# Six input tiles in three passes, an earlier softplus and norm rows in partition halves, in a two-block transformer kernel

## The chip, the cores and the metric

One core of one Trainium2 chip runs the whole program. The metric is the device time in microseconds (us) of one launch, as the median of several runs; lower is better. Engines are called by their short names: PE is TensorE (PEld its weight loads), DVE is VectorE, ACT is ScalarE, POOL is GpSimd, and SP issues the DMAs of the weights. Every engine works through its own list of instructions in program order; a semaphore holds one back until another engine is done.

## What is computed

Two transformer blocks on 256 tokens of width 1024, all in float32. The change touches only the mixer of the second block. Cut to what matters:

```python
u = _rms(h, ln_mix_g)
p = u @ w_in                                   # 1024 x 3384
p_rwkv, p_mla, p_gdn = _split(p, (RWKV_IN, MLA_IN, GDN_IN))
y = concat([rwkv7_time_mix(p_rwkv, ...),       # 6 heads of 64
            mla_attention(p_mla, ...),         # 4 "latent" heads, 96 wide, softmax
            gated_deltanet(p_gdn, ...)])       # 6 heads of 64
h = h + y @ w_out

# in gated_deltanet
q, k, v = split(silu(causal_conv4(qkv)))       # q, k, v from nine input tiles of 128 columns
q, k = l2norm(q) * HEAD_DIM ** -0.5, l2norm(k) # per head and token
g = -exp(a_log) * softplus(a + dt_bias)        # the step sizes, 6 heads x 256 tokens
o = chunked_delta_rule(q, k, v, beta, g)
o = _rms(o, o_norm_g) * silu(gate)             # per head and token
```

The rwkv part has two more such norms per head and token: of its keys (`kk`) and of its output (a group norm).

## The kernel before, in words

**Products.** A product of float32 operands is made in one of two ways. `product_f` (its matmuls are line 626) multiplies the float32 weights with the float32 operand directly, eight matmuls per tile of 128 columns; the profile shows two records for each. `product3` (line 669) works on operands that were split before into a high and a low part of type fp32r: high by high, high by low, low by high, 24 matmuls per tile. The high part is made by an ACT copy, the low part by a DVE subtraction. Most weights are split in pieces (`split_high`, line 1645, and `split_low`, line 2217). The operand of the second block's input product is split too (`stream2`, IN_HIGH and IN_LOW), but its last chunks, in2 3 to 6, are used unsplit.

**The latent heads.** The four softmax heads (units NU to NU+3) run in a loop over u with the names below. What each engine does for step u, in its order:
- PE: `scores` of head u (L798), `probs_T` of head u-1 (three transposes, L839), `filler`, one input tile of chunks in2 4 and 5 (`product_f`, 128 columns, eight matmuls), and `values` of head u-1 (L845 to L847). Fillers 0 to 5 stand in front of and in this loop; tiles 6 and on follow behind it.
- ACT: the conv's first tap of a finished tile (L1695, with a copy of the tile, L1666), `take_probs_T` (L1794), `exps` (L1784, two Exp with sums), `conv_tanh` (L1703); at u = NU, NU+1, NU+2 a step of the softplus on 6x256 or 6x128 numbers: Exp (L2008), Ln (L2011), two Exp (L2014).
- DVE: `bias_scores` (L2379, L2381), `conv_taps` (three, L2261), `conv_out` (L2270), `finish_head` (L2420), and `delta_rule_rows`, which is the DVE's side of the softplus (L2721, L2722, L2726, then L2729 to L2733 with two scans); at u = NU also `key_factors` (L2746 to L2753).

Each engine's list is written out by hand; buffers are double (`u % 2`), so DVE waits for ACT's tap and tanh and ACT for DVE's mask within a step.

**Behind the loop.** `kk_r` are the norm factors of the keys, spread over the heads' rows by PE (`spread_rows`, L1146) and multiplied in by DVE (L2772). DVE then goes through decay factors, conv tiles and the first matrices of the triangular inverse without a break up to the masks of `by_k` (L2981); PE's `removed_values` (L1227) waits for these. From there the inverse runs level by level: PE makes products "p" (L1384), ACT copies them (L1718), PE makes "t", DVE adds (L2825) and transposes (L2832). Between p and t of a level stands `part(lv)`: for the rwkv inverse `spread_rows` of the norms of q and k (levels 2 and 3, DVE L2870 and L2876); after level 4 of the second inverse, `gn_r`.

**Norm rows.** A norm is: squares; `row_sums` (L1095), which sums each head's 64 rows with six matmuls of 32 output rows, three for tokens 0 to 127 into rows 0 to 31 and then three for tokens 128 to 255 into rows 32 to 63; a Sqrt on ACT (L1973) and a reciprocal on DVE; `spread_rows`, six matmuls from 64 rows, which place the factors on 128 rows again, tile by tile.

**The output product.** Fills and jobs are PSUM banks with a fixed order. `out2(dc, tt, ks)` adds the products of the mixer's eight tiles k (0 to 2 rwkv, 3 and 4 latent, 5 to 7 delta rule) for token half tt and column half dc. Tiles 5 to 7 exist last: DVE multiplies by `o_r` (L3013), ACT makes the high parts (L2134), DVE the low parts (L3007), tile by tile; out2(0, ...) takes k = 4 to 7 with both token halves under each k.

## Time and profile before

| | us |
|---|---|
| runs, median of 3 (lowest, highest) | 958.39 (958.37, 959.28) |
| profiled execution, its own time | 958.64 |
| its span from the first to the last instruction | 956.8 |
| PE busy, matmuls (PEld, weight loads) | 935.7 (829.5) |
| DVE busy | 589.0 |
| ACT busy | 471.9 |
| POOL busy | 61.9 |
| mean granted TensorE clock, share of full | 0.998 |
| the latent heads' loop and what follows up to L1227 | about 610 to 669 |
| the levels of the two inverses | about 666 to 741 |
| output product of the mixer | about 741 to 774 |

Busy is the time in which the engine works on an instruction; the times of the span count from its start. A line of the timeline gives the start, the duration (of a whole run of like instructions, where it ends in a count), and in brackets how long the engine had stood idle before, with what released it.

### The profile page before, as it was taken

The page shows a single profiled execution, that of the slowest core. Times are in us where ns is not written, and L with a number is a line of the kernel's source. Part 1 is how long each engine was busy: PE and PEld are TensorE (multiplying, and loading weights), DVE is VectorE, ACT ScalarE, POOL GpSimd, SP SyncE. Part 2 cuts the span into 40 slices and gives each one's busy share as a digit, 9 for nine tenths or more (in the row PEclk, how much of TensorE's full clock was granted, in tenths as well). Part 3 has the DMA queues.
Part 4 walks back from the last instruction along what each step waited for, and adds up shares of the span by engine and source line. Part 5 has one row for each costly group of instructions (what it writes and reads, how often), then busy time and mean ns, then how long its engine had stood idle before and what let it go on. Part 6 is the DMA issues. An engine that isn't in the chain of part 4 may idle for free.

```text
span 956.8 us, 16842 instructions
## 1 busy us (share of the span) xinstructions
PE 935.7 (98%) x7117; PEld 829.5 (87%) x7117; DVE 589.0 (62%) x933; ACT 471.9 (49%) x709; POOL 61.9 (6%) x78
## 2 busy tenths in 40 slices
PE   6999999999999999999999999999999999999998
PEld 5999987787778789999988889887988789998886
DVE  4775445557678755555544669578767466665434
ACT  5644335546774445444453584556336455454331
POOL 1000000020002300000000000002350000000000
PEclk9999999999999999999999999999999999999999
DMA  9985552234346534444554432222000444455521
GB/s 354 202 323 186 192 197 103 107 123 163 131 174 257 189 149 177 177 176 177 185 193 172 182 132 113 89 89 89 3 2 12 167 177 176 177 186 199 215 104 45
DMA packets 14778, 149.86 MB, mean 157 GB/s; under 512 B 1696, under 2 KB 3872, under 8 KB 6128
## 3 DMA queue, kind: packets, MB, share of 16 engines
q1 hardware_dynamic: 12448, 139.65, 39.3%
q0 software_dynamic: 1296, 5.24, 2.9%
q10 hardware_dynamic: 960, 3.90, 1.1%
q8 instruction: 57, 0.93, 0.4%
q14 instruction: 17, 0.14, 0.0%
HBM read 144.59 MB, written 4.19 MB: 155 GB/s over the span
## 4 chain that ended last, share of the span: by engine, by line
PE 83%; DVE 7%; ACT 4%; issue 2%; POOL 1%; ACTq 0%; DVEq 0%; POOLq 0%
PE bank L669 63%; PE bank L626 5%; PE bank L1384 3%; DVE W_LOW L2217 3%; ACT W_HIGH L1645 2%; PE bank L798 1%; POOL HN L3102 1%; PE bank L839 1%; PE bank L876 1%; PE bank L1146 1%; DVE ARENA L2261 1%; DVE X L2523 1%; PE bank L1251 1%; DVE OUT_LOW L2217 0%; PE bank L635 0%
## 5 line engine op out<-in xcount | busy, mean ns | idle before, releaser
L2217 DVE TENSOR_TENSOR W_LOW<-weights,W_HIGH 128x2048 fp32r<-128x2048 f32 (+1 forms) x98 | 224.4, 2292 | 212.2 <-ACT W_HIGH L1645 212.2
L1645 ACT ACTIVATE W_HIGH<-weights 128x2048 fp32r<-128x2048 f32 (+1 forms) x98 | 186.7, 1907 | 262.9 <-PE bank L669 262.9
L669 PE MATMUL bank<-OVER_HT,W_HIGH 128*128 128x256 f32 x608 | 171.0, 281 | 0.3 <-DVE OVER_HN L2229 0.3
L669 PE MATMUL bank<-OVER_HN,W_HIGH 128*128 128x256 f32 x608 | 170.5, 280 | 0.0
L669 PE MATMUL bank<-OVER_HT,W_LOW 128*128 128x256 f32 x608 | 170.5, 280 | 0.0
L669 PEld LDWEIGHTS bank<-OVER_HT,W_HIGH 128*128 128x128 f32 x608 | 114.5, 188 | 1.0 <-issue 0.7
L669 PEld LDWEIGHTS bank<-OVER_HN,W_HIGH 128*128 128x128 f32 x608 | 114.5, 188 | 0.0
L669 PEld LDWEIGHTS bank<-OVER_HT,W_LOW 128*128 128x128 f32 x608 | 114.5, 188 | 0.0
L669 PE MATMUL bank<-W_LOW,HID_HIGH 128*128 128x512 f32 x200 | 77.9, 389 | 0.0
L669 PE MATMUL bank<-W_HIGH,HID_LOW 128*128 128x512 f32 x200 | 77.8, 389 | 0.0
L669 PE MATMUL bank<-W_HIGH,HID_HIGH 128*128 128x512 f32 x200 | 77.8, 389 | 0.0
L669 PE MATMUL bank<-FIRST_HIGH,W_HIGH 128*128 128x256 f32 x224 | 63.6, 284 | 2.0 <-DVE W_LOW L2217 1.4
L669 PE MATMUL bank<-FIRST_HIGH,W_LOW 128*128 128x256 f32 x224 | 63.4, 283 | 0.0
L669 PE MATMUL bank<-FIRST_LOW,W_HIGH 128*128 128x256 f32 x224 | 63.3, 283 | 0.0
L626 PE MATMUL bank<-HT,weights 128*128 128x256 f32 x240 | 55.4, 383 | 0.0
L669 PE MATMUL bank<-GATE_HIGH,FIRST_HIGH 128*128 128x512 f32 x128 | 52.5, 410 | 0.5 <-DVE RING_LOW L2357 0.5
L669 PE MATMUL bank<-RING_LOW,FIRST_HIGH 128*128 128x512 f32 x128 | 50.3, 393 | 0.0
L626 PEld LDWEIGHTS bank<-HT,weights 128*128 128x128 f32 x240 | 44.5, 190 | 6.7 <-issue 0.7
L669 PE MATMUL bank<-GATE_HIGH,FIRST_LOW 128*128 128x512 f32 x128 | 50.2, 392 | 0.0
L2357 DVE TENSOR_TENSOR RING_LOW<-weights,GATE_HIGH 128x1024 fp32r<-128x1024 f32 x32 | 40.7, 1271 | 11.9 <-ACT GATE_HIGH L1680 11.9
L669 PEld LDWEIGHTS bank<-FIRST_HIGH,W_HIGH 128*128 128x128 f32 x224 | 42.3, 189 | 3.4 <-DVE W_LOW L2217 1.8
L669 PEld LDWEIGHTS bank<-W_HIGH,HID_HIGH 128*128 128x128 f32 x200 | 37.5, 188 | 7.8
(513 smaller groups left out, 1873.7 us busy)
## 6 DMA issues: line engine op xcount, KB each, us to landing
weights<-weights_dram SPq DMA_DIRECT2D x63, 2048.0 KB, 8.0
bias_rows_dram<-ARENA POOLq DMA_DIRECT2D x1, 3072.0 KB, 40.5
weights<-weights_dram SPq DMA_DIRECT2D x2, 1024.0 KB, 5.8
BIAS<-params_dram ACTq DMA_DIRECT2D x1, 1997.0 KB, 14.3
weights<-weights_dram SPq DMA_DIRECT2D x1, 1664.0 KB, 6.6
weights<-weights_dram SPq DMA_DIRECT2D x1, 1584.0 KB, 6.8
X<-x_dram ACTq DMA_DIRECT2D x2, 512.0 KB, 4.4
HT<-bias_rows_dram POOLq DMA_DIRECT2D x1, 1024.0 KB, 9.9
```

Of the source, the lines that this page charges most:

```text
L626: ins = pe.matmul(o, w[:, k, a:a + n], HT[:, k, :], start=(k == 0), stop=(k == KD - 1))
L669: ins = pe.matmul(o, left[a][k], right[b][k], start=(first and k == 0 and a + b == 0), stop=(last and k == n - 1 and a == 1))
L798: ins = pe.matmul(BK[4 + u % 2][:, c0:c1], q[:, q0:q0 + P], k[:, 0:n], start=True, stop=(br != 2))
L839: ins = pe.transpose(probsT_bank(u)[:, j * P:(j + 1) * P], PB_[:, u % 2, j * P:(j + 1) * P], ident)
L876: ins = pe.matmul(o[pb:pb + HD, c0:S], V[:, n, a:a + HD], PT_[:, u % 2, k0:k1], start=(n == 0), stop=(n == 1))
L1146: ins = pe.matmul(o[:, c * P:(c + 1) * P], at[0:HD, :], rows, start=True, stop=True)
L1251: ins = pe.matmul(o[pb:pb + HD, c * P:(c + 1) * P], a[:, c, h * HD:(h + 1) * HD], b[:, matrix(c, h), :], start=(n == 0), stop=(c == 0 and ...
L1384: ins = pe.matmul(o[b:b + HD, n * HD:(n + 1) * HD], left[b:b + HD, 4 * g + n, :], right[b:b + HD, 4 * g + n, :], start=True, stop=True)
L1645: act.activation(like_source(piece_parts(k)[0], k), piece_source(k), ACT.Copy).then_inc(sem("pieces_high"), 1)
L2217: dve.tensor_tensor(low, piece_source(k), high.bitcast(F32), ALU.subtract)\
L2261: ins = dve.scalar_tensor_tensor(out=a, in0=o[:, 0:S - d], scalar=w[tap], in1=a, op0=ALU.mult, op1=ALU.add)
L2357: dve.tensor_tensor(low, src, high.bitcast(F32), ALU.subtract).then_inc(sem("gate_split"), 1)
```

## The change

**Tiles.** Input tiles 0 to 5 of chunks in2 4 and 5 (fillers 0 to 5) are made by `product3`. For tile n ACT copies the high part into one of two buffers TILE_HIGH0 and TILE_HIGH1 (`tile_high`, 128x1024), DVE writes the low part over the weights themselves (`tile_low`, 128x1024, into RING_LOW). Tiles 0 and 1 are split in front of the loop, tiles 2 to 5 at the head of steps 0 to 3: tile n + 2 waits until PE has read tile n.

**Softplus.** Both first steps of the softplus (DVE rows and Exp, Ln) move in front of the loop, followed by an Exp on one number.

**Norm rows.** Sums take 64 output rows per token half, in turns between the halves; the root and the reciprocal work on 128 rows; `spread_rows` reads token half c from rows 64c to 64c+63 and writes it to a bank of its own, in turns between the two. The DVE instructions that use the factors go by token halves (128x3x128) and not by tiles. One ACT copy that made a second set of selectors goes away; one of 32x384 remains.

**Output product.** `o_r` is used by token halves: two multiplications, two high parts, two low parts. out2(0, ...) takes k = 4 for both token halves, then k = 5 to 7 for the first and then for the second.

```diff
+        IN_TILES = 6
+        TILE_HIGH = [over("TILE_HIGH0", "HN", 0, [KD, P]), over("TILE_HIGH1", "BIAS", Y_RW_AT, [KD, P])]
...
             def row_sums(o, src):
-                for c in range(2):
-                    for t in range(3):
-                        ins = pe.matmul(o[32 * c:32 * c + 32, :], HEADS[:, 32 * t:32 * t + 32], src[:, t, c * P:(c + 1) * P],
+                for t in range(3):
+                    for c in range(2):
+                        ins = pe.matmul(o[HD * c:HD * (c + 1), :], HEADS[:, HD * t:HD * (t + 1)], src[:, t, c * P:(c + 1) * P],
                                         start=(t == 0), stop=(t == 2))
...
-                ins = product_f(o[:, t * S:(t + 1) * S], w, (n % 4) * P)
+                if n < IN_TILES:
+                    pe.wait_ge(sem("tiles_split"), n + 1)
+                    ins = product3(o[:, t * S:(t + 1) * S], [[part[:, k, :] for k in range(KD)] for part in in_tile(n)[0:2]],
+                                   [[part[:, k, :] for k in range(KD)] for part in stream2])
...
             def spread_rows(names, rows):
-                for o, t, last in tile_slots(names):
-                    for c, at in enumerate((prm2("pair_rows", t * P, P), LATE_ROWS[:, t * P:(t + 1) * P])):
-                        ins = pe.matmul(o[:, c * P:(c + 1) * P], at[0:HD, :], rows, start=True, stop=True)
+                banks = open_halves(*names)
+                for t in range(3):
+                    for c, o in enumerate(banks):
+                        half = slice(c * HD, (c + 1) * HD)
+                        ins = pe.matmul(o[:, t * P:(t + 1) * P], prm2("pair_rows", t * P, P)[half], rows[half],
+                                        start=True, stop=True)
...
-            for k in range(4, KD):
-                for tt in range(TT):
-                    out2(0, tt, (k,))
+            for tt in range(TT):
+                out2(0, tt, (4,))
+            for tt in range(TT):
+                out2(0, tt, range(5, KD))
...
             def tile_high(n):
+                slot, turn = weight_slots("in2", 4 + n // 4)
+                act.wait_ge(sem(f"weights_in{slot}"), 16 * turn)
+                if n >= 2:
+                    wait_tile_read(act, n - 2)
+                high, _, src = in_tile(n)
+                act.activation(high[:, :, :], src, ACT.Copy).then_inc(sem("tiles_high"), 1)
...
             act.activation(BETA, BETA, ACT.Tanh, scale=0.5).then_inc(sem("beta_tanh"), 1)
+            act.wait_ge(sem("sp_minus_abs"), 2)
+            act.activation(GSPT, GSPT, ACT.Exp).then_inc(sem("sp_exp"), 1)
             for n, dst in enumerate((QTm, KTm)):
                 for b in range(2):
                     take_fill(("mla_T", 2 * n + b), flat(dst[0:QK, 2 * b:2 * b + 2, :]), 512, rows=QK)
+            act.wait_ge(sem("sp_exp1"), 2)
+            act.activation(GSPT, GSPT, ACT.Ln).then_inc(sem("sp_ln"), 1)
+            act.activation(SPARE, SMALL[0], ACT.Exp)
             for u in range(NU, NU + MH + 1):
+                if u < NU + IN_TILES - 2:
+                    tile_high(u - NU + 2)
...
+            delta_rule_rows(NU)
+            delta_rule_rows(NU + 1)
             for u in range(NU, NU + MH + 1):
                 if u < NU + MH:
                     bias_scores(u)
+                if u < NU + IN_TILES - 2:
+                    tile_low(u - NU + 2)
...
+            for c in range(2):
+                o = fill_arrived(dve, ("o_r", c))
+                fill_out(dve.tensor_tensor(token_half(Y_GD, c), token_half(GKB, c), three_tiles(o), ALU.mult), ("o_r", c))
+            for c in range(2):
+                dve.wait_ge(sem("y2_high"), 3 + c)
+                dve.tensor_tensor(token_half(OVER_HT[:, 5:8, :], c), token_half(Y_GD, c),
+                                  token_half(OVER_HN[:, 5:8, :], c).bitcast(F32), ALU.subtract).then_inc(sem("y2_split"), 1)
```

The order of instructions on ACT between the tanh of beta (L1991 before, L2035 in the change) and the first two Exp with sums of the loop (L1784 before, L1818 in the change), first before, then in the change. L1718 and L1752 are the copies of the transposed queries and keys:

```order
L1991 ACTIVATE SM<-SM 6x256 [waits beta_in]
L1718 ACTIVATE ARENA<-bank 96x512 [waits fills_written] x4
L1784 ACTIVATE ARENA,STAT<-ARENA,STAT 128x128 [waits probsT_written,scores_read]
L1784 ACTIVATE ARENA,STAT<-ARENA,STAT 128x256
L2008 ACTIVATE SM<-SM 6x256 [waits sp_minus_abs]
```

```order
L2035 ACTIVATE SM<-SM 6x256 [waits beta_in]
L2037 ACTIVATE SM<-SM 6x256 [waits sp_minus_abs]
L1752 ACTIVATE ARENA<-bank 96x512 [waits fills_written] x4
L2042 ACT_TABLE_LOAD
L2042 ACTIVATE SM<-SM 6x256 [waits sp_exp1]
L2043 ACT_TABLE_LOAD
L2043 ACTIVATE STAT<-STAT 128x1
L2021 ACTIVATE TILE_HIGH_57<-weights 128x1024 [waits tiles_read,weights_in1]
L1818 ACTIVATE ARENA,STAT<-ARENA,STAT 128x128 [waits probsT_written,scores_read]
L1818 ACTIVATE ARENA,STAT<-ARENA,STAT 128x256
```

Two table loads, the Ln, the one-number Exp and the high part of tile 2 now stand ahead of the first head's exponentials; before, both loads came in the loop's steps 1 and 2.

DVE at the start of the loop, before and in the change. The two ISA rows that name a bank are the masks of a head's scores (L2379 and L2381 before, L2425 and L2427 in the change), RECIPROCAL is the first instruction of `key_factors`:

```order
L2379 ISA ARENA,STAT<-bank,CST 128x128 [waits job_out0,probs_ready,scores_written,residual_scaled]
L2379 ISA STAT 128x1
L2381 ISA ARENA,STAT<-bank,CST 128x256
L2381 ISA STAT 128x1
L2721 TENSOR_SCALAR SM<-SM 6x256 [waits beta_tanh]
L2722 SCALAR_TENSOR_TENSOR SM<-SM 6x256
L2746 RECIPROCAL HN<-HN 64x128 [waits fill_out4]
```

```order
L2775 TENSOR_SCALAR SM<-SM 6x256 [waits job_out0,beta_tanh,residual_scaled]
L2776 SCALAR_TENSOR_TENSOR SM<-SM 6x256
L2780 TENSOR_SCALAR SM<-SM 6x256 [waits sp_exp]
L2425 ISA ARENA,STAT<-bank,CST 128x128 [waits probs_ready,scores_written]
L2425 ISA STAT 128x1
L2427 ISA ARENA,STAT<-bank,CST 128x256
L2427 ISA STAT 128x1
L2759 TENSOR_TENSOR RING_LOW_50<-weights,TILE_HIGH_57 128x8x128 [waits tiles_high]
L2800 RECIPROCAL HN<-HN 128x128 [waits fill_out4]
```

The low part of tile 2 stands between the first head's masks and `key_factors`, and waits for ACT's high part; the same instruction, for tiles 3 to 5, stands behind the masks of heads 1 to 3.

## Rows read from the trace of the kernel before

**Rows 1.** The page: busy time of each engine, and the chain that ended last, by engine.

```profile
PE 935.7 (98%) x7117; PEld 829.5 (87%) x7117; DVE 589.0 (62%) x933; ACT 471.9 (49%) x709; POOL 61.9 (6%) x78
PE 83%; DVE 7%; ACT 4%; issue 2%; POOL 1%; ACTq 0%; DVEq 0%; POOLq 0%
```

**Rows 2.** Stretches: length, busy us (xcount) of PE, PEld, DVE, ACT, POOL; clock, DMA, GB/s.

```profile
615.00:641.00 26.00, 26.00 (x147) 23.31 (x146) 19.46 (x60) 14.86 (x39) 0.00 (x0) 1.00 0.25 95
641.00:668.00 27.00, 26.05 (x250) 21.94 (x248) 24.07 (x52) 17.18 (x39) 5.59 (x8) 1.00 0.22 79
684.00:700.00 16.00, 16.00 (x275) 14.70 (x275) 12.50 (x31) 9.18 (x21) 5.93 (x6) 0.89 0.01 2
```

**Rows 3.** Timeline of PE: start us, us, engine line op out<-in xcount [idle before <-releaser].

```profile
668.96 1.62 PE L1227 MATMUL bank<-HN,ARENA 128*64 128x64 f32 x48 [1.29 <-DVE ARENA L2981]
```

**Rows 4.** Timeline of PE: a product_f tile (16 records), and product3 matmuls 24 apart.

```profile
614.98 3.62 PE L626 MATMUL bank<-HT,weights 128*128 128x256 f32 x16
...
583.25 0.28 PE L669 MATMUL bank<-IN_LOW,W_HIGH 128*128 128x256 f32 x1
...
586.13 0.28 PE L669 MATMUL bank<-IN_LOW,W_HIGH 128*128 128x256 f32 x1
```

**Rows 5.** One line each: 128x1024 high and low parts elsewhere; then two low parts on end.

```profile
L1680 ACT ACTIVATE GATE_HIGH<-weights x32: 1040/1057/1063, 136.2 to 270.5; 128x1024 fp32r<-128x1024 f32 x32
L2357 DVE TENSOR_TENSOR RING_LOW<-weights,GATE_HIGH x32: 1214/1224/1776, 139.2 to 274.4; 128x1024 fp32r<-128x1024 f32 x32
...
768.68 4.48 DVE L2217 TENSOR_TENSOR W_LOW<-weights,W_HIGH 128x2048 fp32r<-128x2048 f32 x2
```

**Rows 6.** Timeline of ACT: copies before the loop, and the softplus's Ln between two table loads.

```profile
610.96 2.00 ACT L1718 ACTIVATE ARENA<-bank 96x512 f32<-96x512 f32 x4
...
622.77 1.28 ACT L2011 ACT_TABLE_LOAD   x1
624.40 0.42 ACT L2011 ACTIVATE SM<-SM 6x256 f32<-6x256 f32 x1 [0.35 <-DVE SM L2726]
...
625.86 1.28 ACT L1784 ACT_TABLE_LOAD   x1
```

**Rows 7.** Timeline of DVE in the loop of the latent heads and just behind it.

```profile
615.28 0.29 DVE L2379 CUSTOM_DVE_ANT_0 ARENA<-bank,CST 128x128 f32<-128x128 f32 x1 [4.74 <-PE bank L798]
...
616.04 0.40 DVE L2722 SCALAR_TENSOR_TENSOR SM<-SM 6x256 f32<-6x256 f32 x1
...
628.48 0.42 DVE L2270 SCALAR_TENSOR_TENSOR ARENA<-ARENA 128x256 f32<-128x256 f32 x1 [1.74 <-ACT ARENA L1703]
...
632.36 1.52 DVE L2261 SCALAR_TENSOR_TENSOR ARENA<-ARENA,BIAS 128x255 f32<-128x255 f32 x3 [1.07 <-ACT ARENA L1695]
...
639.40 1.14 DVE L2772 TENSOR_TENSOR ARENA<-ARENA,bank 128x512 f32<-128x512 f32 x2 [0.59 <-PE bank L1146]
```

**Rows 8.** Timeline of PE and DVE around spread_rows of the norms of q.

```profile
673.45 0.49 PE L1146 MATMUL bank<-HN,BIAS 64*128 64x128 f32 x2
...
674.98 3.02 PE L1384 MATMUL bank<-ARENA 64*64 64x64 f32 x96
...
674.64 1.02 DVE L2870 SCALAR_TENSOR_TENSOR ARENA<-ARENA,bank 128x512 f32<-128x512 f32 x2 [1.05 <-PE bank L1146]
```

**Rows 9.** Timeline of PE: other matmuls from 64-row halves, four of 128 and twelve of 256.

```profile
653.73 0.71 PE L1183 MATMUL bank<-ARENA 64*128 64x128 f32 x8 [0.61 <-ACT HN L1718]
...
663.26 2.86 PE L1211 MATMUL bank<-ARENA 64*128 64x256 f32 x24
```

**Rows 10.** Timeline: row_sums of the delta rule's output; the reciprocal of gn_r on DVE.

```profile
756.05 1.09 PE L1095 MATMUL bank<-ARENA,NF 128*32 128x128 f32 x12
...
726.75 0.94 DVE L2945 RECIPROCAL HN<-HN 64x128 f32<-64x128 f32 x1 [1.32 <-ACT HN L1973]
```

**Rows 11.** Timeline of DVE and PE in the output product.

```profile
761.24 0.75 DVE L3013 TENSOR_TENSOR HT<-ARENA,bank 128x256 f32<-128x256 f32 x2 [2.72 <-PE bank L1146]
...
767.62 0.50 PE L669 MATMUL bank<-OUT_HIGH,OVER_HN 128*128 128x512 f32 x1 [0.18 <-DVE OUT_LOW L2217]
```

More of the change, by code:

```diff
@@ L430, in wait_job_out, with in_tile, wait_tile_read @@
             eng.wait_ge(sem(f"job_out{j % 4}"), j // 4 + 1)
+        def in_tile(n):
+            slot = weight_slots("in2", 4 + n // 4)[0]
+            cols = slice(n % 4 * P, (n % 4 + 1) * P)
+            src, low = [t[:, :].rearrange("p (k n) -> p k n", k=KD)[:, :, cols] for t in (rings[slot], RING_LOW[slot])]
+            return TILE_HIGH[n % 2], low, src
+        def wait_tile_read(eng, n):
+            if n % 2:
+                eng.wait_ge(sem("jobs_written"), JOB_AT["in2", 4 + n // 4, n // 2 % 2] + 1)
+            else:
+                eng.wait_ge(sem("tiles_read"), n // 2 + 1)
         def piece_parts(k):
@@ L2708, in _, with tile_low @@
             ins.then_inc(sem("rates_low"), 1)
+            def tile_low(n):
+                dve.wait_ge(sem("tiles_high"), n + 1)
+                high, low, src = in_tile(n)
+                dve.tensor_tensor(low, src, high[:, :, :].bitcast(F32), ALU.subtract).then_inc(sem("tiles_split"), 1)
             shift_tiles(3, 0, (8, 9))
+            for n in range(2):
+                tile_low(n)
             shift_tiles(3, 1, (10,))
```

95 lines of the change are left out of this document (42 added, 53 removed).

## The prediction, made before the kernel was run

> **What bounds the kernel now.** I read the page first. PE is busy for 98% of the span and holds 83% of the chain that ended last [rows 1], so a microsecond taken off PE should count, unless another engine is as full in that place. So I read each stretch by itself. In the latent heads' loop (615 to 641) PE is never idle and DVE is busy 19.46 of 26 us, with 6.5 us idle in small waits. Behind it (641 to 668) DVE is busy 24.07 of 27 [rows 2], and at its end PE stands still for 1.29 us until DVE has masked the `by_k` matrices [rows 3]. So from the loop to L1227 both engines are nearly full, and the last wait ends on DVE: PE time saved there is worth only what DVE can follow. The change takes work off PE and puts new work on DVE and ACT in just this place. From L1227 on PE leads again: DVE waits 1.05 us for `spread_rows` [rows 8].
>
> **Tiles, the PE side.** A `product_f` tile takes 3.62 us [rows 4]. In `product3` 24 matmuls start within 2.88 us (583.25 to 586.13), the last ending 0.16 later than the step: 3.04 us. Saved: 0.58 a tile, 3.5 for six.
>
> **Tiles, the DVE and ACT side.** A high part of 128x1024 takes ACT 1.06 us, a low part DVE 1.22 [rows 5]; two low parts on end take 4.48 where one of 2.28 is listed, so the next starts 0.1 before the end, and I take 1.13 a low part. Tiles 0 and 1 fall into idle time in front of the loop (DVE then waits 4.74 us for the first scores [rows 7]) and cost nothing; if they did delay anything it would be by their 2.3 us, but 4.74 covers them. Tiles 2 to 5 add 4 x 1.13 = 4.5 us to DVE within the loop.
>
> **Softplus.** Three DVE rows leave the loop, the longest 0.40 us [rows 7]; I take 0.85 for all (0.2 to 1.2). On ACT the Exp now comes before the four copies and waits for the tanh and two DVE rows: copies that began at 610.96 [rows 6] begin about 0.9 later and end at 613.9. Then come a table load (1.28), Ln (0.35), a table load (1.28) and the small Exp (0.1): 616.9, and with tile 2's high part (1.06) 617.95. In front of the loop the shorter `row_sums` gives 0.2 and tile 0 0.6, but PE's first scores need the copies, so DVE's loop starts only 0.2 us earlier than at 615.28. Its masks are done at 615.6, and it waits until 617.95 for the high part: a **new wait of 2.35 us**, with `key_factors` and the next head's masks queued behind it, for which ACT's second exponentials and then PE's `probs_T` wait.
>
> **The loop, as DVE's account.** From the first masks to the keys' norms are 24.1 us (615.28 to 639.40 [rows 7]). Out: rows -0.85; the wait of 1.74, which is the table loads of Ln in steps 1 and 2, back to the usual 0.5 for a tanh, -1.2; the 1.07 for a tap, -1.05; the 0.59 for `spread_rows`, -0.6, since PE is ahead of DVE there; two small waits for PE and ACT, -0.65. In: low parts +4.5; the wait at tile 2 +2.35; at tile 5 about +1.35, because its high part stands on ACT behind two Exp (size of the Ln's 0.42 [rows 6]) that wait for DVE's scans, so 0.8 + 1.06 less the 0.55 us of masks. Sum +3.85, less the 0.2 at the start: +3.65. From there to L1227 DVE has no slack, except that the product of `by_k` is waited for less, as PE gains on DVE: -0.45. **To L1227: +3.2 us.** PE's 3.5 saved become idle time, mostly in front of `probs_T` and `values`. Bounds: 2.3, if each signal costs 0.04 less than I count; 4.3 with the full 1.22 and 1.06.
>
> **Norm rows.** No row shows six 128-column matmuls in turns between row halves. Four (L1183) take 0.71 us, 0.35 a pair. Twelve of 256 columns (L1211), six pairs, take 2.86, 0.48 a pair, so a pair of 128 columns would take 0.24 [rows 9]. Three pairs: 0.7 to 1.05; I take 0.88, nearer to the value of L1183, as three short pairs are more like two than like six of double length. Now it takes 1.53 (673.45 to 674.98 [rows 8]), so 0.65 less each (0.45 to 0.8; zero if the halves do not run side by side). `gq_r` and `gk_r`: 1.3, less 0.2 as DVE's share of a level (its 1.02 for the factors and two groups of three) becomes the longer at the second: -1.1. `gn_r`: DVE arrives through ACT's table load and root (its wait of 1.32 is on ACT [rows 10]) and has no idle time behind it, so half counts: -0.3. `kk_r` is in the account above. TensorE: Matmul & The Clock Gate of the Trainium skill (section on array packing by 32x32 tiles) has small-K matmuls in distinct row groups run fully side by side; three pairs would then take about 0.65 (its rule with the 0.2 that a matmul of 128 columns takes alone, an estimate), and the sum would be 0.7 us lower than mine; the trace agrees only in part, with 0.35 and 0.24 a pair.
>
> `row_sums`: 1.09 us now [rows 10] in 32-row outputs; I take 0.2 less for the turns (0 to 0.45), which counts at the last one only; the others are covered by DVE, or by ACT's root. Root, reciprocal and the halved DVE instructions have as many elements per row and cost what they did. One ACT copy of 32x384 and a larger memset on POOL lie before the loop, where POOL has nothing else and ACT waits; I count nothing for them, and 0.4 at most if ACT were full there. SP's next loads wait for the same jobs as before and are for the output product, some 100 us later: nothing.
>
> **Output product.** PE reaches it 0.85 us earlier (0.2 + 0.65). It now needs tile k = 5 of the first token half 1.5 us after `spread_rows`; the chain DVE 0.47, ACT 0.42, DVE 0.5 and three signals is 1.75, so PE waits some 0.2. The 0.18 for the last low part [rows 11] goes, because ACT has two high copies rather than three in front of it. Sum -0.9 (-0.3 to -1.2). If the chain is longer, the work hidden now behind four matmul groups shows.
>
> **The sum.** +3.2 - 1.1 - 0.3 - 0.9 = **+0.9 us**. The profiled execution took 958.64, 0.25 above the median of 958.39; from the median: **959.3 us**. About 0.2% (1.9 us) is what a measurement of this kernel can tell from no change, so this reads as none.
>
> **Rivals.**
> *PE leads in the loop after all* (chance 0.2). If DVE's low parts fit into its 6.5 idle us [rows 2] and the wait at tile 2 does not come, each of steps 0 to 4 is shorter by PE's 0.58, and L1227 comes 3.1 earlier: 959.3 - 3.2 - 3.1 = 953.0. For it: PE's share of the page, and enough idle time by number. Against: the idle pieces are round trips with ACT that stay, and the loads stand in front of tile 2.
> *Slower: the halves do not run side by side* (0.13). If three pairs take as long as six matmuls (1.53), or DVE proves the longer in the levels too, the 1.1, 0.3 and 0.65 of 0.9 are lost, 2.05 in all, and the 3.2 stand: 961.4. It decides from about 1.4 us for three pairs. For it: two pairs of L1183 are 40% dearer than long ones. Against: L1211.
> *The clock falls* (0.12). In 684 to 700 the granted clock is 0.89 of 2.4 GHz on average [rows 2], that is 3.5 us at the 1.2 GHz level, 1.75 us of work, with PE busy throughout. PE will now stand still for over 3 us in step 3. One such stretch more in a place where PE leads costs 1.75: 961.05; inside the loop, DVE covers it. If the stretch at 694 goes instead, the same amount is gained (957.5, which reads as no change; I give it a third of this chance).
> *Dearer table loads* (0.05). In the trace Ln follows 1.63 us after the start of its load, 0.35 of it a wait for DVE, so a switch costs 1.28 [rows 6]; the loads of the first step then cost 2.56 and the wait 2.35. If a switch took twice that, the new wait would be 4.9 and the time 961.9. ScalarE: Activation LUTs of the Trainium skill (What ACT_TABLE_LOAD costs) gives 1.38 us of draining beside 1.28 of loading per switch, 2.66 together; that would be 962.1, and the trace disagrees.
> *The rest*, 0.5, is my forecast, with its own range 957.6 to 961.2 from the bounds above.
>
> **Chances.** Faster by over 0.2% (below 956.5): the first rival and the edge of mine, 0.22. Slower (above 960.3): the halves 0.13, the clock 0.08, the table loads 0.05 and 0.1 of mine, 0.36, put at 0.35. Same: the rest, 0.43. The range has to leave out 0.2: that is the first rival in full. Its low end, 955.6, lies a little under the middle between 959.3 and 953.0, for a loop in which PE leads in some steps only; its high end is the dearest of the others, 961.9.
>
> **What would show it.** Right: a DVE wait of 2 to 3 us for TILE_HIGH before the first `key_factors`, one of about 1.3 before the last; the keys' norms (L2772's place) 3 to 4 us later than 639.40; L1227 about 3.2 us later, still released by DVE; PE idle several us in the loop; `spread_rows` 0.8 to 1.0 us long; the output product starting about 1.8 later than before and its end 0.9. Wrong: L1227 earlier than 668.96; a DVE wait under 1 us at tile 2; PE without idle time in the loop; or `spread_rows` at 1.5.

## The result, and the profile after

| | before | after |
|---|---|---|
| runs, median (lowest, highest), 18 each | 958.52 us (956.93, 960.95) | 960.69 us (959.01, 962.94) |
| ratio, 95% interval | | 1.0021 (1.0013 to 1.0029) |
| profiled execution (span) | 958.64 us (956.8) | 960.36 us (958.5) |

The change makes the kernel slower by 0.21%, 2.0 us by the ratio (2.2 between the medians); the interval, 0.13 to 0.29%, lies about the bound of 0.2% for "no change". The forecast was 959.3, +0.9 us.

The page of the changed kernel, busy time and chain, against [rows 1]:

```profile
PE 930.4 (97%) x7165; PEld 825.1 (86%) x7165; DVE 595.9 (62%) x937; ACT 476.7 (50%) x714; POOL 62.1 (6%) x78
PE 79%; DVE 10%; ACT 6%; issue 3%; POOL 1%; ACTq 0%; DVEq 0%; POOLq 0%
```

PE lost 5.3 us of work and 4 points of the chain; DVE and ACT, which gained 6.9 and 4.8 us, took them over. The stretches, with the columns of [rows 2]:

```profile
615.00:641.00 26.00, 21.13 (x146) 19.68 (x145) 20.48 (x52) 14.67 (x38) 0.00 (x0) 0.88 0.22 82
641.00:668.00 27.00, 26.02 (x215) 22.18 (x216) 22.35 (x45) 17.48 (x39) 4.41 (x6) 0.99 0.21 79
684.00:700.00 16.00, 16.00 (x317) 14.70 (x314) 12.29 (x31) 8.51 (x19) 4.50 (x4) 1.00 0.01 3
```

In the loop PE is idle for 4.9 of 26 us, where it was never idle, and its clock is 0.88: a part of the loop runs at the 1.2 GHz level. The low stretch that the kernel before had behind 694 us is gone here.

**A common zero first.** The two profiles part before the first changed instruction. A table load of ACT behind a long run of `product3` matmuls, and a read of DVE at the head of the part that this case is about, first before, then after:

```profile
486.46 1.28 ACT L1584 ACT_TABLE_LOAD   x1
570.30 0.16 DVE L2628 TENSOR_SCALAR STAT<-bank 128x2 f32<-128x2 f32 x1 [1.36 <-PE bank L1040]
```

```profile
485.04 1.28 ACT L1618 ACT_TABLE_LOAD   x1
568.90 0.16 DVE L2674 TENSOR_SCALAR STAT<-bank 128x2 f32<-128x2 f32 x1 [1.89 <-PE bank L1063]
```

The profiled execution after is 1.40 us ahead at 570, by work that is the same in both. A second step of this kind lies behind 780 us (last section), so the ends of two spans can't be compared either. Therefore, below, "against before" means the difference of the times of one and the same instruction, plus 1.40; for other kernels, plus what they were ahead at this read.

Timeline of DVE after, through the loop, against [rows 7]:

```profile
613.71 0.29 DVE L2425 CUSTOM_DVE_ANT_0 ARENA<-bank,CST 128x128 f32<-128x128 f32 x1 [2.78 <-PE bank L821]
...
616.75 1.23 DVE L2759 TENSOR_TENSOR RING_LOW<-weights,TILE_HIGH 128x1024 fp32r<-128x1024 f32 x1 [2.40 <-ACT TILE_HIGH L2021]
...
633.88 1.23 DVE L2759 TENSOR_TENSOR RING_LOW<-weights,TILE_HIGH 128x1024 fp32r<-128x1024 f32 x1 [1.18 <-ACT TILE_HIGH L2021]
...
642.70 0.17 DVE L2466 RECIPROCAL STAT<-STAT 128x2 f32<-128x2 f32 x1 [1.75 <-PE bank L870]
...
643.56 1.14 DVE L2831 TENSOR_TENSOR ARENA<-ARENA,bank 128x384 f32<-128x384 f32 x2 [0.37 <-PE bank L1178]
```

The first masks come 0.17 earlier against before (613.71 - 615.28 + 1.40 = -0.17; forecast 0.2). The waits at tiles 2 and 5 are 2.40 and 1.18 (forecast 2.35 and 1.35). The third wait, 1.75 for L870, the values of head 3, is not in the forecast, and the keys' norms are 5.56 late (643.56 - 639.40 + 1.40) where 3.65 were forecast. Timeline of PE around that wait, and the same time in stretches of 2 us (columns of [rows 2]):

```profile
635.10 0.69 PE L868 MATMUL bank<-ARENA 128*128 128x64 f32 x2 [2.87 <-ACT ARENA L1828]
635.59 0.63 PE L869 MATMUL bank<-ARENA 128*128 128x64 f32 x2
...
637.94 0.41 PE L692 MATMUL bank<-IN_LOW,TILE_HIGH 128*128 128x256 f32 x1
...
641.88 0.33 PE L868 MATMUL bank<-ARENA 128*128 128x64 f32 x2
```

```profile
632.00:634.00 2.00, 0.23 (x2) 0.02 (x1) 0.82 (x6) 1.81 (x4) 0.00 (x0) 1.00 0.71 303
634.00:636.00 2.00, 0.90 (x4) 0.90 (x5) 1.97 (x3) 1.93 (x7) 0.00 (x0) 0.66 0.00 0
636.00:638.00 2.00, 2.00 (x12) 2.00 (x12) 1.45 (x6) 1.09 (x3) 0.00 (x0) 0.50 0.00 0
638.00:640.00 2.00, 2.00 (x11) 2.00 (x11) 1.86 (x5) 0.18 (x1) 0.00 (x0) 0.50 0.00 0
640.00:642.00 2.00, 2.00 (x14) 2.00 (x13) 0.46 (x2) 0.42 (x1) 0.00 (x0) 0.63 0.04 8
```

PE stood still for 2.87 us in front of the values of head 2. While it did, the clock fell to 1.2 GHz and stayed there until about 641.4. Tile 5 then took 4.94 us (636.94 to 641.88) instead of some 3.0, a matmul of 128x256 0.41 instead of 0.28, and the values of head 3 behind it came when DVE had long been ready. What PE had waited for is in ACT's list:

```profile
632.19 0.41 ACT L2059 ACTIVATE SM<-SM 6x256 f32<-6x256 f32 x1 [2.35 <-DVE SM L2787]
632.51 0.39 ACT L2060 ACTIVATE SM<-SM 6x128 f32<-6x128 f32 x1
632.81 1.04 ACT L2021 ACTIVATE TILE_HIGH<-weights 128x1024 fp32r<-128x1024 f32 x1
...
634.59 0.46 ACT L1828 ACTIVATE ARENA<-bank 128x384 f32<-128x384 f32 x1
```

L1828 copies the transposed probabilities of head 2. In front of it stand two Exp that wait for DVE's scans and the high part of tile 5.

Behind the loop: PE at L1260 (L1227 before, [rows 3]), and at the norms of q (L1178, [rows 8]); DVE's factors for q; the output product [rows 11].

```profile
672.91 1.62 PE L1260 MATMUL bank<-HN,ARENA 128*64 128x64 f32 x48 [1.29 <-DVE ARENA L3037]
...
677.40 0.94 PE L1178 MATMUL bank<-HN,BIAS 64*128 64x128 f32 x12
678.27 3.17 PE L1417 MATMUL bank<-ARENA 64*64 64x64 f32 x96
...
765.25 0.47 PE L692 MATMUL bank<-OUT_HIGH,OVER_HN 128*128 128x512 f32 x1 [0.35 <-DVE OVER_HT L3066]
```

```profile
678.37 1.02 DVE L2928 SCALAR_TENSOR_TENSOR ARENA<-ARENA,bank 128x384 f32<-128x384 f32 x2 [0.82 <-PE bank L1178]
...
741.70 2.29 DVE L2263 TENSOR_TENSOR OUT_LOW<-weights,OUT_HIGH 128x2048 fp32r<-128x2048 f32 x1
...
766.83 2.29 DVE L2263 TENSOR_TENSOR OUT_LOW<-weights,OUT_HIGH 128x2048 fp32r<-128x2048 f32 x1 [1.26 <-ACT OUT_HIGH L1679]
```

L1260 is still released by DVE, with the same wait of 1.29. `spread_rows` takes 0.87 us for 1.53. From the keys' norms on, the lead of the kernel before shrinks: 5.56 at the norms, 5.35 at L1260, 3.92 at the split at 741.70 (739.18 before) and 2.96 at that of 766.83 (765.27 before).

### The profile page after: what moved, and what is told of

Its sections match the earlier page's. It is cut to its first block, busy times and chain, and to the rows that moved or that the text cites. A ratio compares the mean times of both kernels' runs of the same rounds, so it can differ in the third digit from the quotient of the medians.

```text
span 958.5 us, 16955 instructions
## 1 busy us (share of the span) xinstructions
PE 930.4 (97%) x7165; PEld 825.1 (86%) x7165; DVE 595.9 (62%) x937; ACT 476.7 (50%) x714; POOL 62.1 (6%) x78
## 4 chain that ended last, share of the span: by engine, by line
PE 79%; DVE 10%; ACT 6%; issue 3%; POOL 1%; ACTq 0%; DVEq 0%; POOLq 0%
PE bank L692 63%; PE bank L1417 3%; DVE W_LOW L2263 3%; PE bank L649 2%; ACT W_HIGH L1679 2%; DVE ARENA L2307 1%; POOL HN L3150 1%; PE bank L821 1%; PE bank L862 1%; PE bank L899 1%; DVE X L2569 1%; PE bank L1284 1%; DVE OUT_LOW L2263 0%; PE bank L1178 0%; PE bank L658 0%
## 5 line engine op out<-in xcount | busy, mean ns | idle before, releaser
L692 PEld LDWEIGHTS bank<-W_HIGH,HID_LOW 128*128 128x128 f32 x200 | 37.5, 188 | 7.9
L692 PEld LDWEIGHTS bank<-W_LOW,HID_HIGH 128*128 128x128 f32 x200 | 37.5, 188 | 7.9
```

Source lines behind the costliest of these rows:

```text
L692: ins = pe.matmul(o, left[a][k], right[b][k], start=(first and k == 0 and a + b == 0), stop=(last and k == n - 1 and a == 1))
```

## The experiments

Twelve kernels were run, each timed in five rounds beside the kernel before, four at a time on one chip. Each is the changed kernel with an edit. Two times of each profile are in this table, both "against before" as above: DVE's product just behind the keys' norms (640.58 before), and its split of an output piece (739.18 before). The last columns say where a profile shows the clock below 0.9, and the ratio of the times.

```
kernel                    640.58   739.18   clock low at     ratio (95%)
norm_rows_only            -0.44    -2.07    -                0.9975 (0.9965 to 0.9986)
norm_rows_softplus        -0.31    -0.63    694-702          0.9972 (0.9962 to 0.9982)
two_tiles                 -0.93    -2.55    694-698          0.9976 (0.9966 to 0.9986)
two_tiles_softplus_back   -1.39    -1.58    702-706          0.9962 (0.9949 to 0.9975)
reordered4                -0.62    -2.25    -                0.9977 (0.9968 to 0.9987)
reordered                 +1.90    +0.27    636-640          0.9990 (0.9982 to 0.9999)
high2_early               +1.96    +0.53    634-638, 696-700 0.9999 (0.9990 to 1.0007)
softplus_back             +2.53    +2.33    628-636, 706-710 1.0011 (1.0002 to 1.0019)
five_tiles                +4.00    +2.38    634-638          1.0011 (1.0001 to 1.0021)
pe_kept_busy              +3.27    +3.13    706-710          1.0011 (1.0003 to 1.0020)
tiles_parts_unused        +3.49    +1.86    -                1.0022 (1.0012 to 1.0032)
the change                +5.56    +3.92    634-642          1.0021 (1.0013 to 1.0029)
norm_rows_undone          +5.96    +7.44    634-642, 710-714 1.0050 (1.0032 to 1.0067)
```

### Which part costs: norm rows alone, with the softplus, with six tiles

```diff
-        IN_TILES = 6
+        IN_TILES = 0
...
-            act.wait_ge(sem("sp_minus_abs"), 2)
-            act.activation(GSPT, GSPT, ACT.Exp).then_inc(sem("sp_exp"), 1)
...
-            act.wait_ge(sem("sp_exp1"), 2)
-            act.activation(GSPT, GSPT, ACT.Ln).then_inc(sem("sp_ln"), 1)
-            act.activation(SPARE, SMALL[0], ACT.Exp)
...
-                if u == NU + 2:
+                if u == NU:
+                    act.wait_ge(sem("sp_minus_abs"), 2)
+                    act.activation(GSPT, GSPT, ACT.Exp).then_inc(sem("sp_exp"), 1)
+                elif u == NU + 1:
+                    act.wait_ge(sem("sp_exp1"), 2)
+                    act.activation(GSPT, GSPT, ACT.Ln).then_inc(sem("sp_ln"), 1)
+                elif u == NU + 2:
...
-            delta_rule_rows(NU)
-            delta_rule_rows(NU + 1)
...
-                if u > NU + 1:
-                    delta_rule_rows(u)
+                delta_rule_rows(u)
```

> The changed kernel with no split tile (all input tiles by product_f) and the softplus back in the loop: what is left is the norm rows and the output product. By my account these are worth 0.5 us at the keys' norms (the 0.59 that DVE waited for spread_rows), 1.1 at the norms of q and k, 0.3 at gn and 0.65 in the output product: 2.5 us below the kernel before, about 956.0, with no clock below 2.4 GHz in the loop. If the row halves do not gain (the rival), it is within 0.5 us of before. If the step of 1.4 us between 355 and 486 us, in code that the change does not touch, belongs to the changed program and not to the execution, this profile shows it too; if it belongs to the execution, it is there or not by chance.

Measured: 956.54 us, ratio 0.9975, 2.4 us faster. The norm rows and the output product are worth what the account gave them. The zero of this profile is 0.15, so the 1.40 of the change's profile does not come with the norm rows.

`norm_rows_softplus` has `IN_TILES = 0` alone and keeps the softplus in front.

> As the run before, but with the softplus in front of the loop. By my account DVE loses 0.85 us of rows and 1.2 us of a wait for the Ln's table loads in the loop, and the two loads stand in front of the first exponentials, which come about 0.9 us later: 0.5 to 1.5 us faster than the run with the norm rows alone, about 955.0. If the loads in front cost as much as those in the loop, no difference.

Measured: 956.04 us, ratio 0.9972, no measurable difference to the run before; at the keys' norms it is 0.13 later. The expected gain did not come: DVE's waits for the Ln are gone, but it then waits 1.11 and 1.41 us for values of PE. The rival held.

`softplus_back` has the other hunks and keeps six tiles.

> The changed kernel with the softplus back in the loop, six tiles split. Account: the wait of 2.35 us at tile 2 goes, the rows (0.85) and the wait for the Ln (1.2) come back: within 0.5 us of the changed kernel (960.2 to 961.2) if the clock falls as before, and about 958.5 if ACT's other order keeps PE from standing still for 2.9 us in front of the values of head 2, so that the clock does not fall. The rival that the table loads are what makes the change slow expects 958 as well, but with an idle PE and a low clock still there.

Measured: 959.69 us, ratio 1.0011, about 1 us below the change, between the cases. PE still stood idle, 2.31 us, one step earlier, and the clock fell there. In this place DVE did cover the fall: none of its waits up to the keys' norms is for PE. What it waits for is ACT, whose Ln and its table load now hold up the high part of tile 4 (1.11 us), and tile 5 (1.18).

```profile
628.06 0.69 PE L868 MATMUL bank<-ARENA 128*128 128x64 f32 x2 [2.31 <-ACT ARENA L1828]
```

The last of the parts, all but the norm rows and the output product:

```diff
             def spread_rows(names, rows):
-                banks = open_halves(*names)
-                for t in range(3):
-                    for c, o in enumerate(banks):
+                for o, t, last in tile_slots(names):
+                    for c, at in enumerate((prm2("pair_rows", t * P, P), LATE_ROWS[:, t * P:(t + 1) * P])):
...
```

> The changed kernel with the norm rows and the output product as they were: six split tiles and the softplus in front remain. Theory (the parts add up: norm rows and output product are worth 2.4 us, tiles with softplus cost the rest): 2.0 to 2.5 us above the changed kernel, about 0.45% above before (962.5 to 963.2). The profile should show the same DVE waits at tiles 2 and 5, PE idle for about 2.9 us and the low clock behind it. Rival (the change's parts interact, and the norm rows' gain came from what the loop left open): within 1 us of the changed kernel.

Measured: 963.23 us, ratio 1.0050, 2.8 us above the change. `spread_rows` of q takes its old 1.53 us. The parts add up: norm rows and output product bring 0.25% alone and 0.29% here (1.0050 to 1.0021); six tiles with the softplus cost 0.46% on top of them (0.9975 to 1.0021) and 0.50% by themselves. The profile has DVE's waits at tiles 2 and 5 (2.39 and 1.18), PE's idle time (2.87) and the low clock behind it, as expected.

### Is it PE's idle time and the clock

In `pe_kept_busy` PE repeats tile 4's product behind tile 4:

```diff
                 filler(u - NU + 1)
+                if u == NU + 3:
+                    product3(job_bank(("in2", 5, 0))[:, S:2 * S], [[part[:, k, :] for k in range(KD)] for part in in_tile(4)[0:2]],
+                             [[part[:, k, :] for k in range(KD)] for part in stream2])
```

> The changed kernel, with 24 more matmuls behind tile 4, which fill the 2.87 us in which PE waited for ACT's copy in front of the values of head 2; they repeat tile 4's product into the half of the bank that tile 5 then writes over, so the result is unchanged. Theory (the clock fell after this idle time, tile 5 then took 4.9 us instead of 3.0 and DVE waited 1.75 us for the values of head 3): granted clock 1.0 throughout the loop, the wait of 1.75 below 0.3, time 1.5 to 2.0 us below the changed kernel (958.7 to 959.2). Rival (DVE's own work sets the end of the loop and the wait is only taken over by the next one): clock 1.0 but a time within 0.5 us of the changed kernel.

Measured: 959.93 us, ratio 1.0011, about 1.0 us below the change, less than expected. In the loop the theory held. The clock is 1.0, DVE does not wait for the values of head 3, and the keys' norms come 2.3 us earlier than in the change; timelines of DVE and PE:

```profile
640.56 0.33 PE L868 MATMUL bank<-ARENA 128*128 128x64 f32 x2
...
642.22 0.16 DVE L2469 RECIPROCAL STAT<-STAT 128x2 f32<-128x2 f32 x1
```

In this profile the rest went behind 706 us, where it has a low stretch that the change's has not. The first table prices it: from 640.58 to 739.18 every profile without a low stretch in between gains 1.62 to 1.64 us (norm_rows_only, reordered4, reordered, five_tiles, tiles_parts_unused, the change), and the four with one beyond 700 only 0.14 to 0.32. So a stretch there costs 1.3 to 1.5 us. One that is over by 700 costs 0.2 (`high2_early`) or nothing (`two_tiles`; the kernel before has its own in the same place), as DVE leads there. But the stretch at 706 is not why the kernel gained only 1.0 us: its five executions at a mean clock of 1.000 have a median of 960.47, its six at 0.998 one of 959.52. Executions at full clock lie 2.8 us apart here (957.93 to 960.74), which is more than a fall costs. The two speeds of the last section can make up to 2.4 us of that; which execution had which, only a trace would tell. So the gain in time that the theory forecast, 1.5 to 2.0 us, is not shown, though its mechanism in the loop is.

Second, in `tiles_parts_unused` ACT and DVE do all of their splitting, but tiles 2 to 5 are `product_f` again, over the low parts (so this part of the output is not the reference's):

```diff
-                    ins = product3(o[:, t * S:(t + 1) * S], [[part[:, k, :] for k in range(KD)] for part in in_tile(n)[0:2]],
-                                   [[part[:, k, :] for k in range(KD)] for part in stream2])
+                    if n < 2:
+                        ins = product3(o[:, t * S:(t + 1) * S], [[part[:, k, :] for k in range(KD)] for part in in_tile(n)[0:2]],
+                                       [[part[:, k, :] for k in range(KD)] for part in stream2])
+                    else:
+                        low = in_tile(n)[1].bitcast(F32)
+                        ins = product_f(o[:, t * S:(t + 1) * S], low, 0)
```

> The changed kernel, where tiles 2 to 5 are multiplied by product_f again, as before, while ACT and DVE make their high and low parts all the same (the product is taken with the low parts, so this part of the output is not the reference's). PE has 4 x 0.58 = 2.3 us more work in the loop, ACT's and DVE's lists are unchanged. Theory (PE's saving within the loop buys nothing, since DVE sets the time there and the saved time is idle time that also lets the clock fall): no slower than the changed kernel, and 0.5 to 1.5 us faster if the idle time of 2.87 us shrinks so far that the clock stays at 2.4 GHz. Rival (PE's work counts in the loop): 1 to 2.3 us slower than the changed kernel, 961.5 to 963.

Measured: 960.19 us, ratio 1.0022, the change's within the noise. PE does 2.3 us more in the loop, and it costs nothing that the times show. Its profile is the change without a low clock:

```profile
635.09 0.43 PE L868 MATMUL bank<-ARENA 128*128 128x64 f32 x2 [2.29 <-ACT ARENA L1832]
```

```profile
641.04 0.29 DVE L2471 TENSOR_TENSOR NF<-bank,STAT 128x128 f32<-128x128 f32 x1
...
641.48 1.14 DVE L2835 TENSOR_TENSOR ARENA<-ARENA,bank 128x384 f32<-128x384 f32 x2
```

DVE's list up to the masks of head 3 is that of the change (its waits at tiles 2 and 5 are 2.40 and 1.19), and the keys' norms are 3.49 late instead of 5.56: the clock's share of the change's loop is 2.07 us by this pair of profiles, 2.29 by that of `pe_kept_busy`. The theory also expected a faster kernel, and it is not: its other executions fell about as often as the change's. This table has the mean granted clock of every timed execution (0.999 counted with 1.000; before, in the three sets that ran beside the experiments); 0.998 is about one stretch of some 3.5 us at half speed in 957, 0.996 two or a longer one:

```
                        executions   1.000   0.998   under 0.998
before (three sets)             83      49      24            10
the change                      18       0       4            14
tiles_parts_unused              12       2       3             7
high2_early                     11       1       2             8
softplus_back                   11       0       4             7
norm_rows_undone                 6       1       2             3
reordered                       11       1       8             2
five_tiles                      12       1       8             3
pe_kept_busy                    12       5       6             1
norm_rows_only                   7       5       2             0
norm_rows_softplus               7       3       3             1
two_tiles                        9       4       4             1
reordered4                      12       6       3             3
two_tiles_softplus_back          6       3       3             0
```

No execution of the change kept its clock, and 14 of 18 lost the longer time; before, 10 of 83, of which 8 in the set of 23 that ran beside `tiles_parts_unused`. In the change the executions under 0.998 have a median of 961.3, the four at 0.998 one of 959.4; in `tiles_parts_unused` those under 0.998 have 961.3, the others 959.6. So sorted by clock the two kernels take the same time, and the clock is worth some 1.7 to 2.0 us in both. The profiled execution of `tiles_parts_unused` (959.23, its fastest) is one of its two clean ones. Where in the span the others fell, no trace shows. A profile of one execution shows where a fall may be and what it costs, not how often it comes.

### Places against amount

> The changed kernel with IN_TILES = 2: only tiles 0 and 1, whose parts are made in front of the loop; norm rows and softplus as in the change. Theory (the tiles split within the loop are what costs: their low parts and the two waits for high parts, and the clock after PE's idle time; tiles 0 and 1 are free): the time of the run with norm rows and softplus alone (956.0) less 0.6 for tile 1, since tile 0 only makes PE wait for ACT's copies: about 955.5. Rival (splitting as such is dear, by ACT and DVE time in front of the loop too): 956.5 or more.

The edit of `two_tiles` is `IN_TILES = 2`. Measured: 956.21 us, ratio 0.9976: 4.3 us below the change, so what costs is in tiles 2 to 5; the other two are not dear, but the 0.6 that the profile shows at the keys' norms did not come through in the times.

```diff
+            tile_high(2)
             act.wait_ge(sem("sp_exp1"), 2)
...
-                if u < NU + IN_TILES - 2:
+                if NU < u < NU + IN_TILES - 2:
                     tile_high(u - NU + 2)
```

> The changed kernel with the high part of tile 2 made ahead of the Ln's two table loads instead of behind them. Theory: DVE's wait of 2.40 us at tile 2 goes (its low part then starts right behind the first masks), ACT's first exponentials start where they did, and DVE's list runs up to 2.3 us earlier, unless it then waits for the probabilities that follow the exponentials: 1.0 to 2.3 us below the changed kernel, 958.4 to 959.7. The idle time of PE in front of the values of head 2, and the low clock after it, may stay, since they come from the wait of ACT for the two scans. Rival (PE's idle time and the clock are the whole of the loss): no difference.

Measured: 958.20 us, ratio 0.9999, 2.1 us below the change. The wait at tile 2 is gone; the wait at tile 5 (1.19), PE's idle time (2.57) and the clock are still there. A wait of 2.40 us was worth 2.1.

> The changed kernel with tile 5 unsplit (IN_TILES = 5). In step 3 ACT's high part (1.04 us), DVE's wait for it (1.18) and the low part (1.13) go, and the copy for the values of head 2 comes 1 us earlier. Theory: the idle time of 2.87 us becomes about 1.8, DVE gains 2.3 us in step 3 and waits for the values of head 3 instead, which come behind a tile 5 of 3.5 us at full clock, or of 5 us or more at half: with full clock 2.0 to 2.5 us faster than the changed kernel (958.3), with the clock falling all the same 0.5 to 1 us faster. Rival (the loss sits at tile 2): within 0.5 us of the changed kernel.

The edit is `IN_TILES = 5`. Measured: 959.49 us, ratio 1.0011, 1.0 us below the change. PE's idle time is 1.93 us, and the clock falls all the same: the lesser of the two gains foreseen.

```diff
+                if NU < u < NU + IN_TILES - 2:
+                    tile_high(u - NU + 2)
                 if u > NU:
                     conv_tanh(u - NU + 7)
-                if u == NU + 2:
+                if u == NU + 3:
                     act.wait_ge(sem("gdn_cumulated"), 1)
...
-                if u < NU + IN_TILES - 2:
-                    tile_low(u - NU + 2)
+                if u == NU and IN_TILES > 2:
+                    tile_low(2)
                 if u > NU:
                     conv_taps(u - NU + 7)
+                    if u < NU + IN_TILES - 2:
+                        tile_low(u - NU + 2)
                     conv_out(u - NU + 7)
```

This is `reordered`, with the hunk that makes high part 2 early; `reordered4` has `IN_TILES = 4` besides.

> All six tiles, norm rows and softplus as in the change, in another order: the high part of tile 2 ahead of the table loads; high parts 3 to 5 behind the exponentials of their step, low parts 3 to 5 between the conv's taps and its output, where DVE otherwise waits 0.48 us for a tanh; ACT's two Exp for the decay behind the exponentials of head 3, so that they no longer hold up the copy for the values of head 2. Theory (the loss is in the places, not in the amount of work): no wait of DVE over 1 us in the loop but for PE, PE idle less than 1.5 us in it and the clock at 1.0; 954.5 to 956.0, below the run with norm rows and softplus alone. Rival (four low parts on DVE are worth more than four times 0.58 us of PE wherever they stand): 956.5 to 958.5.

> The run reordered with four tiles split (0 to 3). Theory: PE is 1.16 us slower than with six, DVE 2.26 us shorter in steps 2 and 3; if PE leads there this run is up to 1.2 us slower than reordered, if DVE leads up to 2.3 us faster; by the theory that the places decide, within 0.6 us of it.

Measured: 956.93 us, ratio 0.9990, for six tiles: 3.0 us below the change, but by the ratios 1.4 to 1.7 us slower than with none (the intervals meet), and 1.90 late at the keys' norms where those are early. So the rival holds. A new wait took the place of the old, PE for the low part of tile 5, and the clock fell again:

```profile
635.29 0.35 PE L692 MATMUL bank<-IN_HIGH,TILE_HIGH 128*128 128x256 f32 x1 [1.76 <-DVE RING_LOW L2760]
```

With four tiles 955.49, ratio 0.9977, 1.2 us faster than with six (the intervals meet; at the keys' norms the profiles differ by 2.52) and the same as with two or none: not the same as six within 0.6, as the theory of the places had it. Each split tile in the loop asks 1.14 of DVE for 0.58 of PE; by these four counts DVE has room in the loop for about two of them, and they bring nothing.

> Norm rows and output product, tiles 0 and 1 split, softplus back in the loop. The copies of the transposed queries and keys come as early as PE's tile 0 allows, so the first masks come 0.6 us earlier than with the softplus in front (as in softplus_back, 614.57 against 615.1), and the Ln's table loads cost DVE their 1.3 and 0.6 us of waits again. Theory: these nearly cancel; within 0.5 us of two_tiles, ratio 0.997 to 0.9975. Rival (tiles 0 and 1 are worth their 1.16 us of PE once the copies no longer hold up the scores): 1 us below norm_rows_only, ratio 0.9965.

Both edits seen already. Measured: 955.02 us, ratio 0.9962 (0.9949 to 0.9975): 1.2 us below norm_rows_only, as the rival had it; the profiles have 0.95 at the keys' norms. It has six executions only, and its interval meets those of norm_rows_only, norm_rows_softplus, two_tiles and reordered4. The first masks of DVE come 0.80 us earlier against before, in the change 0.17, since ACT's copies are not behind the softplus's Exp:

```profile
614.43 0.29 DVE L2426 CUSTOM_DVE_ANT_0 ARENA<-bank,CST 128x128 f32<-128x128 f32 x1 [4.15 <-PE bank L821]
...
627.29 0.43 DVE L2317 SCALAR_TENSOR_TENSOR ARENA<-ARENA 128x256 f32<-128x256 f32 x1 [1.75 <-ACT ARENA L1737]
```

The old wait for the Ln's load is back (1.75), and it still has the lowest time of all: 0.38% below before and 0.59% below the change, both clear of the noise. It takes of the change the norm rows, the output product and tiles 0 and 1.

## Why the prediction was nearly right, and where it failed

**The loop, DVE's account.** Right in its parts: start -0.17 (forecast -0.2), wait at tile 2 2.40 (2.35), at tile 5 1.18 (1.35). With the clock at 1.0 (`tiles_parts_unused`) the keys' norms are 3.49 late (3.65) and L1227's place 3.28 (3.2). That PE's saving in the loop becomes idle time was right, and that run shows it. In the change's own profile the signs given for the norms (3 to 4 us late), for L1227 (3.2) and for the start and end of the output product (1.8 and 0.9) all missed by some 2 us: it has 5.56, 5.35, 3.92 and 2.96.

**The step that failed** is the sentence on the clock, "inside the loop, DVE covers it". I had seen that PE would stand still for over 3 us in step 3 (it was 2.87), and priced a low clock there at nothing, since DVE led. But values of head 3 stand behind tile 5 in PE's list, and tile 5 grew by 1.9 us; PE's slack against DVE was used up, and DVE waited 1.75. The price was 2.07 us, and the case was not one in eight: none of 18 executions went without a fall, and 14 lost more clock than one short stretch takes, though only the profiled one shows where. The step is not wrong everywhere: in `softplus_back` the fall came one step earlier and DVE covered it. I had counted idle time of PE as free; in this kernel it is paid for by the work behind it.

**Behind the loop.** From the keys' norms to L1260 the account had -0.45 and the profile -0.21. `gq_r` and `gk_r`: from 5.35 at L1260 to 3.92 at 739 with `gn_r`, -1.43 in all, forecast -1.4. `spread_rows` 0.87 (0.88). Output product -0.96 (-0.9), with 0.35 of a wait for tile 5 (0.2). So the sum without a fall of the clock, read from `tiles_parts_unused` at 765.27, is +0.90, the forecast's +0.9; the change's profile has +2.96 there, and the difference is the loop's clock. The +0.90 is a reading at that place and not a time: `tiles_parts_unused` as a kernel is no faster than the change. The ratio gives +2.0. That 960.69 lies in the range of 955.6 to 961.9 is luck in part: its high end was drawn for dearer table loads, which did not come, and the fall in the loop came in their place. How much of the 2.0 us is the clock and how much the speeds of single executions (last section), the medians can't tell.

**The rivals.** PE did not lead in the loop. The halves run side by side in part, 0.87 us for the 1.53 of six matmuls in turn, and norm_rows_undone puts their worth at 2.8 us with the output product. The three pairs at 0.87 are near the estimate from L1183. They are above the 0.65 that the forecast had estimated by the rule of TensorE: Matmul & The Clock Gate of the Trainium skill (Part 3: Packing small matmuls), by which matmuls in distinct row groups run at the same time. Dearer table loads fell as well: behind the load at 612.54 the Ln starts at 613.83, 1.29 later, and the next load's Exp 1.29 after its start:

```profile
612.54 1.28 ACT L2042 ACT_TABLE_LOAD   x1
613.83 0.42 ACT L2042 ACTIVATE SM<-SM 6x256 f32<-6x256 f32 x1
614.27 1.28 ACT L2043 ACT_TABLE_LOAD   x1
615.56 0.20 ACT L2043 ACTIVATE STAT<-STAT 128x1 f32<-128x1 f32 x1
```

The 1.38 us of draining that ScalarE: Activation LUTs of the Trainium skill adds to a switch (What ACT_TABLE_LOAD costs) are not in this trace.

**The softplus.** The account gave the hoist 0.85 and 1.2 us on DVE's side and made it pay with the wait at tile 2. Without split tiles it is worth nothing (0.9972 against 0.9975). With two tiles it seems to cost 0.14% (0.9976 against 0.9962), with six 0.1% (1.0021 against 1.0011), but neither is clear of the noise. The profiles show a cost for two tiles: the copies that it delays on ACT release PE's first scores (PE waits 0.48 us for them in `two_tiles`, not at all in `two_tiles_softplus_back`), and the keys' norms come 0.46 later.

## What to carry to other kernels

Two engines that take turns in a loop cannot be relieved one by one: time taken off the one that waits is idle time, and the operand splitting that buys it is added on the other. Where this leaves TensorE idle for as long as here (1.8 to 2.9 us), ask what stands behind that place in its list, price it at half the clock, and look who waits for it. A copy that releases PE does not belong behind work that waits for a third engine. And a difference under 0.3% is to be read from the timed rounds and, in one profile, against a zero in front of the change.

## What the runs showed of the hardware, unexpected

The clock fell after PE's idle times of 2.87, 2.57, 2.31, 1.93 and 1.76 us in the loop (the change and norm_rows_undone, high2_early, softplus_back, five_tiles, reordered), but not after 2.29 in the one traced execution of `tiles_parts_unused`; what PE had done in front differed there. It also falls with PE busy, at 694 before. What decides it was not tried.

The same products run at two speeds. From 355.30 to 486.46 before and from 355.25 to 485.04 after lies the same work, 131.16 and 129.79 us, with PE hardly idle and the clock at 1.00 in both; the mean of a split matmul is 281 and 280 ns. Five of the 13 profiles of changed kernels are 1.40 to 1.60 us ahead at DVE's read at 570, the others between 0.20 ahead and 0.10 behind, and nothing in the edits sorts them. The same is seen behind the mixer, where DVE's splits follow PE's products. Between two of DVE's splits of weights, first before, then in `tiles_parts_unused`, lie 89.86 and 90.84 us, with PE busy throughout and the clock at 1.00 from 785 to 873:

```profile
783.92 2.29 DVE L2217 TENSOR_TENSOR W_LOW<-weights,W_HIGH 128x2048 fp32r<-128x2048 f32 x1 [3.69 <-ACT W_HIGH L1645]
...
873.78 2.29 DVE L2217 TENSOR_TENSOR W_LOW<-weights,W_HIGH 128x2048 fp32r<-128x2048 f32 x1 [1.15 <-ACT W_HIGH L1645]
```

```profile
783.53 2.29 DVE L2267 TENSOR_TENSOR W_LOW<-weights,W_HIGH 128x2048 fp32r<-128x2048 f32 x1 [3.73 <-ACT W_HIGH L1683]
...
874.37 2.29 DVE L2267 TENSOR_TENSOR W_LOW<-weights,W_HIGH 128x2048 fp32r<-128x2048 f32 x1 [1.18 <-ACT W_HIGH L1683]
```

Seven of the 13 profiles lose this 1.0 us there, the change's (89.90) and five more do not, and it does not go with the step in front. Two spans can thus differ by 2.4 us in parts that are the same in all kernels, at full clock. It seems to belong to the execution, which one profile of each kernel can't settle; its cause is open.
